# A norm folded into the first four units of a gated scan, x loaded in two halves, and low weight parts computed in pieces

## What is computed

```python
def rmsnorm_2(x, gain):
    return x * lax.rsqrt(jnp.mean(x * x, axis=-1, keepdims=True) + EPS) * gain

def hgrn2_mixer(h, w_in, lower_bound, norm_gain, w_o):
    q, f, i, g = jnp.split(h @ w_in, 4, axis=-1)
    q = jax.nn.silu(q)
    forget = lb + (1.0 - lb) * jax.nn.sigmoid(f)
    log_f = jnp.log(forget)
    k = -jnp.expm1(log_f)                      # = 1 - forget
    o = hgrn2_chunk_scan(q, k, i, log_f)       # per head, 8 heads of 128
    return (rmsnorm_2(o, norm_gain) * jax.nn.sigmoid(g)) @ w_o

for layer in range(2):
    h = rmsnorm_2(x, gains[layer, 0])
    x = x + (stick_breaking_mixer(h, ...) if layer == 0 else hgrn2_mixer(h, ...))
    h = rmsnorm_2(x, gains[layer, 1])
    x = x + (relu(h @ w1) ** 2) @ w2           # h: 512x1024, w1: 1024x4096
```

## Time and profile before

| | us |
|---|---|
| runs of the kernel before, median (lowest to highest) | 2004.3 (2002.17 to 2006.76) |
| the profiled execution, its own time | 2006.44 |
| its span in the trace | 2004.3 |
| PE busy | 1958.3 (98%) |
| PE weight loads busy | 1595.7 (80%) |
| DVE busy | 974.2 (49%) |
| ACT busy | 705.0 (35%) |
| POOL busy | 748.6 (37%) |

### The profile page before, as it was taken

One profiled execution on the slowest core, in us unless ns is written; L12 is line 12 of the kernel. 1 busy time (PEld: TensorE's weight loads), 2 busy tenths in 40 slices (PEclk: granted clock), 3 DMA queues, 4 the chain that ended last, 5 costly groups with the idle time before them and its releaser, 6 DMA issues.

```text
span 2004.3 us, 25097 instructions
## 1 busy us (share of the span) xinstructions
PE 1958.3 (98%) x9928; PEld 1595.7 (80%) x9928; DVE 974.2 (49%) x1670; ACT 705.0 (35%) x1129; POOL 748.6 (37%) x308
## 2 busy tenths in 40 slices
PE   7998999999999999999999999999999999999998
PEld 5877777788888877767888888878888888888886
DVE  6648775732225476775522333254755555233332
ACT  4445444543333355564222222232222232222221
POOL 3216222356664322214444444422222145444441
PEclk9989999999999999999999999989999999999999
DMA  6214122223333211112333333222212133333331
GB/s 171 64 33 116 46 59 55 53 69 95 97 104 108 85 53 54 56 41 79 100 95 95 95 95 95 84 74 73 61 56 63 43 85 105 95 95 95 95 95 53
DMA packets 269142, 159.63 MB, mean 80 GB/s; under 512 B 6137, under 2 KB 267489, under 8 KB 269026
## 3 DMA queue, kind: packets, MB, share of 16 engines
q1 hardware_dynamic: 269026, 158.02, 27.3%
HBM read 155.91 MB, written 2.10 MB: 79 GB/s over the span
## 4 chain that ended last, share of the span: by engine, by line
PE 92%; DVE 5%; ACT 1%; issue 1%; DMA 0%; POOL 0%; SPq 0%; ACTq 0%; DVEq 0%
PE bank L244 35%; PE bank L707 6%; PE bank L708 6%; PE bank L709 6%; PE bank L2320 3%; PE bank L2322 3%; PE bank L2321 3%; PE bank L2351 3%; PE bank L1673 3%; PE bank L509 2%; PE bank L1675 2%; PE bank L1674 2%; PE bank L511 2%; PE bank L510 2%; PE bank L879 1%; PE bank L1723 1%
## 5 line engine op out<-in xcount | busy, mean ns | idle before, releaser
L227 POOL TENSOR_TENSOR weight_lo<-weight_stage,weight_hi 128x1024 fp32r<-128x1024 f32 x303 | 748.1, 2474 | 1225.5 <-ACT weight_hi L217 1225.2
L217 ACT ACTIVATE weight_hi<-weight_stage 128x1024 fp32r<-128x1024 f32 x303 | 319.7, 1056 | 326.3 <-PE bank L244 256.7
L2071 DVE TENSOR_TENSOR x_t<-x_t,bank 128x512 f32<-128x512 f32 x128 | 82.3, 684 | 266.7 <-PE bank L244 266.7
L244 PE MATMUL bank<-hidden_hi,weight_lo 128*128 128x512 f32 x512 | 201.9, 394 | 0.0
L707 PE MATMUL bank<-a_hi,weight_lo 128*128 128x512 f32 (+1 forms) x464 | 199.6, 430 | 2.3 <-DVE a_lo_rounded L1211 2.1
L244 PE MATMUL bank<-hidden_hi,weight_hi 128*128 128x512 f32 x512 | 201.8, 394 | 0.0
L244 PE MATMUL bank<-hidden_lo,weight_hi 128*128 128x512 f32 x512 | 201.8, 394 | 0.0
L244 PE MATMUL bank<-a_hi,weight_lo 128*128 128x512 f32 x512 | 199.7, 390 | 0.0
L244 PE MATMUL bank<-a_lo_rounded,weight_hi 128*128 128x512 f32 x512 | 199.3, 389 | 0.0
L244 PE MATMUL bank<-a_hi,weight_hi 128*128 128x512 f32 x512 | 199.2, 389 | 0.0
L708 PE MATMUL bank<-a_lo_rounded,weight_hi 128*128 128x512 f32 (+1 forms) x464 | 184.0, 397 | 0.0
(11 more groups left out here) (341 smaller groups left out, 3557.2 us busy)
## 6 DMA issues: line engine op xcount, KB each, us to landing
weight_stage<-in_mlp_w SPq DMA_DIRECT2D x128, 512.0 KB, 3.9
weight_stage<-in_w_in SPq DMA_DIRECT2D x57, 512.0 KB, 3.8
weight_stage<-in_hg_w_in SPq DMA_DIRECT2D x32, 512.0 KB, 4.0
weight_stage<-in_sb_w_qkv SPq DMA_DIRECT2D x24, 512.0 KB, 3.8
weight_stage<-in_w_mkv SPq DMA_DIRECT2D x8, 512.0 KB, 3.8
weight_stage<-in_w_out SPq DMA_DIRECT2D x8, 512.0 KB, 3.8
weight_stage<-in_sb_w_o SPq DMA_DIRECT2D x8, 512.0 KB, 3.8
weight_stage<-in_hg_w_o SPq DMA_DIRECT2D x8, 512.0 KB, 3.8
```

What stands on the lines that cost most here:

```text
L217: act.activation(self.hi[slot][:, :], self.stage[slot][:, :], ACT.Copy).then_inc(self.hi_done, 1)
L227: pool.tensor_tensor(self.lo[slot][:, :], self.stage[slot][:, :], self.hi[slot][:, :].bitcast(F32), ALU.subtract).then_inc(self.split_done, 1)
L244: last = pe.matmul(out, l, r, start=n == 0, stop=n == 3 * len(pairs) - 1)
L2071: dve.tensor_tensor(S.x[:, t, :], S.x[:, t, :], S.ps[4 + r % 2 * 2 + m][:, :], ALU.add).then_inc(added, 1)
```

## The change

1. The scan's norm becomes a `FoldedNorm` (`ModelNorm` and `Norm` are deleted). In the last four units of the first MLP ACT and DVE make `a_hi`, `a_lo`, squares and their sum tile by tile; the 32 summing matmuls between and behind the units go. PE begins the scan's first unit at once. Its first four units (q0, f0, q1, f1) run on x times gain, into banks 0 to 3. `pe_sums` stands behind unit 0 and `pe_spread` in the middle of unit 1.
2. DVE keeps the factor in `S.sin`, takes out the four results times the factor (`keep_raw`), and multiplies x by gain and factor for all later units (`apply_x`); ACT writes the new high parts over `a_hi` as unit 3 has read them (`raw_read`), and DVE the new low parts (`lower_x`). PE runs the three steps of unit 4 that stood behind the first two scores ahead of them.
3. x is loaded in two halves of 512 columns; the first weight unit is issued behind the first half.
4. `weight_hi` and `weight_lo` are computed only for the columns that a unit has, and POOL's subtraction is done in pieces of 256 columns: 1160 instructions in place of 303. `split_done` is raised by the last piece.

```diff
@@ Weights @@
+PIECE = 256
 def high(self, act, c, i=0, per=0):
...
-        act.activation(self.hi[slot][:, :], self.stage[slot][:, :], ACT.Copy).then_inc(self.hi_done, 1)
+        size = self.units[c][1]
+        act.activation(self.hi[slot][:, 0:size], self.stage[slot][:, 0:size], ACT.Copy).then_inc(self.hi_done, 1)
 def low_units(self, pool, lo, hi):
             pool.wait_ge(self.hi_done, u + 1)
-            pool.tensor_tensor(self.lo[slot][:, :], self.stage[slot][:, :], self.hi[slot][:, :].bitcast(F32),
-                               ALU.subtract).then_inc(self.split_done, 1)
+            for a in range(0, size, PIECE):
+                part = slice(a, min(a + PIECE, size))
+                last = pool.tensor_tensor(self.lo[slot][:, part], self.stage[slot][:, part],
+                                          self.hi[slot][:, part].bitcast(F32), ALU.subtract)
+            last.then_inc(self.split_done, 1)
@@ first_block @@
-            for c in range(4):
-                sp.dma_start(x_tok[:, :, c * 256:(c + 1) * 256],
+            for c in range(2):
+                sp.dma_start(x_tok[:, :, c * T:(c + 1) * T],
...
                 if c == 0:
                     W.load(sp, 0, LAG + 1)
@@ mlp, tensor @@
-                    if later is not None and c == 7 and r >= 1:
-                        later.sum_tile(pe, 2 * r - 2)
-                        later.sum_tile(pe, 2 * r - 1)
@@ mlp, scalar and vector, chunk 7 @@
-                            later.square_tile(act, t)
+                            later.act_tile(act, t)
...
+                        if later is not None and c == 7:
+                            later.dve_tile(dve, t)
@@ hgrn, vector @@
-            norm.dve_apply(dve)
+            def keep_raw(n):
+                kind, h = HG_ORDER[n]
+                dve.wait_ge(W.used, u0 + n + 1)
+                dve.tensor_tensor((qs if kind == "q" else fs)[:, h, :], S.ps[n][:, :], factor[:, :],
+                                  ALU.mult).then_inc(raw_kept, 1)
+            def apply_x(c):
+                dve.scalar_tensor_tensor(out=S.scratch[:, c, :], in0=S.x[:, c, :], scalar=norm.gain_column(c),
+                                         in1=norm.bank[:, :], op0=ALU.mult, op1=ALU.mult).then_inc(x_applied, 1)
+            def lower_x(c):
+                dve.wait_ge(norm.hi_done, norm.tiles + ND + c + 1)
+                dve.tensor_tensor(S.alo[:, c, :], S.scratch[:, c, :], S.ahi[:, c, :].bitcast(F32),
+                                  ALU.subtract).then_inc(norm.lo_done, 1)
+            norm.dve_root(dve)
+            dve.wait_ge(norm.spread_done, norm.spread0 + 1)
+            dve.tensor_copy(factor[:, :], norm.bank[:, :]).then_inc(norm.spread_done, 1)
+            dve.wait_ge(norm.spread_done, norm.spread0 + 2)
+            keep_raw(0)
+            keep_raw(1)
+            for c in range(ND):
+                apply_x(c)
...
             gate_q(0)
             start(0)
+            for c in range(ND - 2):
+                lower_x(c)
+            keep_raw(2)
+            keep_raw(3)
+            for c in (ND - 2, ND - 1):
+                lower_x(c)
             gate_q(1)
             start(1)
@@ hgrn, tensor @@
-            norm.pe_spread(pe)
-            fill(32)
+            begun = quota(0)[0]
+            fill(8)
+            norm.pe_sums(pe)
+            fill(4)
+            norm.pe_spread(pe)
+            fill(20 + begun)
             for h in (0, 1):
                 score(h, 0)
@@ hgrn, scalar @@
-            norm.act_root(act)
-            norm.act_high(act)
-            for n in range(4):
+            for n in range(2):
+                W.high(act, u0 + n + RING)
                 evict(n)
+            W.high(act, u0 + 2 + RING)
+            for c in range(ND):
+                act.wait_ge(x_applied, c + 1)
+                if c < ND - 1:
+                    act.wait_ge(raw_read, c + 1)
+                else:
+                    act.wait_ge(W.used, u0 + 4)
+                    evict(2)
+                    evict(3)
+                act.activation(S.ahi[:, c, :], S.scratch[:, c, :], ACT.Copy).then_inc(norm.hi_done, 1)
+            W.high(act, u0 + 3 + RING)
```

More of the change, by code:

```diff
@@ L642, in first_block @@
         turned_in, copied_in = S.turned, S.copied
-        x_loaded = [S.sem(f"x_loaded{c}") for c in range(4)]
+        x_loaded = [S.sem(f"x_loaded{c}") for c in range(2)]
         RECENT = 5
@@ L1956, in stick_breaking, with mlp @@
         return Stage(sync, gpsimd, tensor, vector, scalar), out
[L1959 removed]
+def mlp(S, layer, norm, later):
     nc, W = S.nc, S.W
[L1961 removed]
     with ExitStack() as scope:
@@ L2111, in hgrn @@
          q_grown, k_grown, scored, picked, k_turned, k_kept, v_turned, v_kept, update,
-         stated, out, out_kept, summed, steps, spread, applied,
+         raw_kept, raw_read, x_applied, stated, out, out_kept, summed, steps, spread, applied,
          gated, out_hi, out_lo) = (S.sem(f"hg_{x}") for x in names)
@@ L2148, in sync @@
         def sync(sp):
-            sp.wait_ge(norm.hi_done, norm.hi0 + 1)
+            sp.wait_ge(norm.hi_done, norm.tiles + 1)
             sp.dma_start(levels[:, :], S.consts[:, K_LEVEL:K_COLS]).then_inc(S.loaded, 16)
@@ L2459, in evict @@
                 bank = proj_banks[n % 2][:, :]
-                act.wait_ge(W.used, u0 + n + 1)
-                if kind == "q":
+                if n < 4:
+                    act.wait_ge(raw_kept, n + 1)
+                else:
+                    act.wait_ge(W.used, u0 + n + 1)
+                if n < 4 and kind == "q":
+                    wait(act, q_gated, h)
+                    act.activation(qsig[:, :], qs[:, h, :], ACT.Sigmoid).then_inc(q_sigmoid, 1)
+                elif n < 4:
+                    act.activation(fs[:, h, :], fs[:, h, :], ACT.Sigmoid).then_inc(f_kept, 1)
+                elif kind == "q":
                     wait(act, q_gated, h)
```

170 lines of the change are left out of this document (52 added, 118 removed).

## The result

The changed kernel runs in 1994.16 us (median of five runs, 1993.18 to 1994.9), the kernel before in 2006.61 beside it (2002.17 to 2007.13). The ratio is 0.9944 [0.9932, 0.9957]: faster, by 11 to 12 us, half of the 23.2 that were forecast. That lies inside the range of 1971 to 1997 and above the forecast's own band of 1975 to 1990. The profiled execution took 1994.9 us, its span is 1993.3.

What follows compares the result with a forecast made beforehand. PE was taken as the bound, busy 1958.3 of 2004.3 us, so gains come only from its idle 46 us, lower clock and 32 small sums. Terms sum to -23.2: 2004.3 to 1981.1 us, range 1971 to 1997.

Steps and rivals of the forecast that it cites:

- A piece on POOL: POOL's subtraction of 256 columns takes 0.60 us, a unit 2.4 (bounds 2.4 to 3.0); each DVE entry costs 0.44.
- Term 3: Pieces beside memory units and first scores: -8.0 from wait and lower clock, +3.2 from POOL; -4.8 us (-8.0 to 0).
- L918 and L1734: PE's waits behind DVE work blocked by POOL shorten with pieces: -2.8 us at L918, -2.9 at L1734.
- L509: PE waits for POOL here, and DVE now enters the subtraction once or twice: +0.6 us (0 to 2.3).
- Term 2: Opening with x in halves: earlier unit 0, no pause at sums, no lower clock from 37.0; -4.8 us (-6.5 to -2).
- the squares' addition ends before PE comes to its sums: Opening: DVE's addition takes 6.5 us with pieces between, so PE's wait of 1.67 us at 34.00 goes.
- L774: PE waits for low parts of a 768-column unit, while DVE has seven two-input products: 0 (-0.8 to +0.8).
- Term 1: Folded norm of the scan: 42.45 us before, 34.0 plus 1.0 for clock after; -7.5 us (-10 to -4).
- Pieces free nothing: Rival: POOL keeps the port from its first piece to its last, blocking DVE; 1998 us, 12%.
- The norm is worth what it removes: Rival: DVE is quicker and PE waits for nothing at the scan's norm, term 13.8 us; 1975 us, 10%.
- POOL the bound: Rival: a piece costs 0.75, a unit 3.0; POOL never catches up beside memory units, PE loses some 7 us; 1987, 20%.
- the third rival: Another name for POOL the bound: PE loses some 7 us in ten memory units in place of 3.2; 20%.

Runs made afterwards that it cites:

- e6: Changed kernel with four of the eight steps of the opening's third unit moved ahead of the sums of squares; 1991.2 us.
- e9: Changed kernel with e6's edit, DVE's adds ahead of gathering in the MLP's last units, and more unit 4 steps ahead of the scan's first scores; 1984.6 us.
- e10: e9 with x loaded in four quarters again instead of halves; 1988.1 us.
- e11: Kernel before with POOL's low parts in pieces alone, x in quarters and norm not folded; 1994.2 us.
- e5: The changed kernel itself run once more as a yardstick; 1998.0 us.
- e14: e9 with the one-column product of score peak and root factor made on ACT instead of DVE; 1984.1 us.
- e15: e14 without the folded norm, the scan's norm as in the kernel before; 1991.8 us.

## Why the prediction was half right

Of the 12.2 us between forecast (-23.2) and span (-11.0), 7.1 are missing at the folded norm, 4.5 up to 136 us and 1.9 at the out projection; the other stretches together gave 1.3 more than forecast.

- **What bounds it.** Right: PE is busy 98% in both, and the 11.0 us are 3.7 of its idle time (46.0 before, 1993.3 - 1951.0 = 42.3 after) and 7.3 of its busy time, which holds the sums and the lower clock.
- **A piece on POOL**, taken at 0.60 between 0.59 and 0.75. With no long entry of DVE it is 0.70, by POOL's unit beside the scan's second (four pieces in 2.79 us):

```profile
1298.79 2.79 POOL L233 TENSOR_TENSOR weight_lo<-weight_stage,weight_hi 128x256 fp32r<-128x256 f32 x4 [3.87 <-ACT weight_hi L221]
```

  The value was taken from the low end of its bounds, because ten whole subtractions had run without a gap. Part of the cost of a further instruction lies inside the instructions, where no gap shows it.
- **Term 3, memory units and first scores**: -5.6 against -4.8, with +2.6 and -8.2 against +3.2 and -8.0. Right in both parts where the product slips through, and that it did in the profiled execution is luck: it is -0.2 together in e6, where it doesn't. The claim that DVE gets in once between two subtractions was read from ten whole ones, and pieces do not keep to it at that product.
- **L918 and L1734**: -6.3 together against -5.7. Right.
- **L509**: +2.5 against +0.6, its bound 2.3. The wait grew from 1.6 to 2.5 and 3.4 us of lower clock came behind it. Where the clock stays (e6, e9, e10, e11) it is +0.9, with the same wait of 2.5.
- **Term 2, the opening**: the failed step is "the squares' addition ends before PE comes to its sums". It was priced at 6.5 us and took 8.1, since each of its seven instructions was held by a piece (8 pieces of POOL stand beside it; seven undisturbed take 4.8). The pause of 1.6 stayed, and the clock that the forecast had back at full was low for 10.2 us. The -1.5 for unit 0 did not come either: PE began at 15.4, not 14.7, and the second unit started at 26.4, where the old kernel's did. In e6, without the pause, the stretch is -5.9. (Half of 3.8 us is 1.9, where the sum has 1.6.)
- **L774, forecast 0** (-0.8 to +0.8): -2.2, and +2.4 in e5. The wait itself grew from 3.7 to 4.4; the rest is how long the clock stayed low around it, 10.2 us before and 6.8 or 17.1 after.
- **Term 1, the folded norm**: the failed step is the clock, priced at 1 us in all and only for the waits at the scores, with 1 us of pause for tile 7. The pause was 2.2, and the clock was low for 6.8 us behind it and for 10.3 at the scores; 39.6 us passed to `score(0, 1)` against the 34.0 taken. "Full clock in unit 0" itself came true, to its last matmuls. DVE's chain from the spread's end (1305.0) to the key of the second head (1326.8) took 21.8 us, forecast 20.6 with nothing in its way and 22.2 for the value taken. But it began 4.4 us late (the spread ended 15.6 us behind the MLP's last matmul, forecast 11.2): 1.4 from the pause for tile 7, the rest from sums, root and half a unit at half clock. Another 3 to 4 us went in the 10.3 us at the second wait and behind it, most of them from `score(0, 1)` on. The prediction's steps to that score, as written, add up to 31.6 and not 32.4; this changes little. e14 against e15 (7.7 by time, 6.9 by stretches) shows the 7.5 us to be there once these pauses are shortened.
- **Rivals.** "Pieces free nothing" is refuted by e11, but what it says of POOL happened to one small product in five of ten profiles. "The norm is worth what it removes" is refuted by -0.4. "POOL the bound" is half seen: a unit of 2.8, but no growth at the memory units beyond the forecast. POOL's waits beside these units are 2.6 us, where the third rival had some 7. None of the rivals named what happened: a pause of PE in the fold's first unit, where none was, with the lower clock behind it, and a second stretch of lower clock at the scores.

## What to carry to other kernels

When a change puts new waits near PE, price each together with the stretch at 1.2 GHz that stands behind waits of its length elsewhere in the same trace: here waits of 2.2 and 4.7 us with the clock behind them left 0.4 us of a gain of 6.9. Take it as a risk and not as a rule: behind the same wait of 2.5 us for POOL at the out projection the clock fell in nine of the thirteen traces with pieces of 256 and stayed in four. Before giving a fold up, look for independent matmuls that can be moved into the pause, and for DVE work that stands ahead of what PE needs. And compare two traces by the starts of the same work: medians of 2000 us could not tell single edits apart, starts that agree within 0.4 us (behind 136 us) could.
